# A decoder layer on one core: expert choice one step later in the dense stage, and a new order of the tail

## What is computed

```python
cat = concatenate([_rms_norm(attn_o, g_attn), _rms_norm(conv_o, g_conv)])
h = _layer_norm(ALPHA * x + cat @ w_out, ln1_g, ln1_b)

scores = sigmoid(h @ router_w)                      # 64 experts, 8 groups of 8
sel = scores + router_bias
gscore = sum(top_k(sel.reshape(T, 8, 8), 2))        # per group
emask = groups among the top 4 by gscore
eidx = top_k(where(emask, sel, -inf), 6)
w = scores[eidx] / sum(scores[eidx]) * 2.5
routed = sum over the six experts of w * (silu(h @ w_gate[e]) * (h @ w_up[e])) @ w_down[e]
shared = (silu(h @ ws_gate) * (h @ ws_up)) @ ws_down
y = _layer_norm(ALPHA * h + routed + shared, ln2_g, ln2_b)
```

## Time and profile before

| | |
|---|---|
| median of 3 runs | 2155.15 us (2153.55 to 2159.5) |
| the profiled execution, its own time | 2160.44 us |
| its span, from first to last instruction | 2158.7 us |
| mean granted TensorE clock | 0.983 of full speed |
| PE busy | 2056.4 us, 95% of the span |
| DVE busy | 1412.8 us, 65% |
| ACT busy | 1244.0 us, 58% |
| POOL busy | 635.8 us, 29% |
| chain that ended last, PE's part | 38% of the span |

### The profile page before, as it was taken

The page is one execution under the profiler, slowest core; times in us unless marked ns, Lnnn a source line. Parts: engine busy times, 40 slices in busy tenths (PEclk is TensorE's granted clock), DMA queues, the critical chain, the costliest instruction groups (busy, mean ns, idle before and its releaser), DMA issues.

```text
span 2158.7 us, 37047 instructions
## 1 busy us (share of the span) xinstructions
PE 2056.4 (95%) x11574; PEld 1728.6 (80%) x11574; DVE 1412.8 (65%) x2788; ACT 1244.0 (58%) x2169; POOL 635.8 (29%) x659
## 2 busy tenths in 40 slices
PE   8999999999989999969999999999999999999984
PEld 6777787787767777758888888898988888888773
DVE  6444444444667777776777777677767777767657
ACT  6344344343543444436777777677667777766655
POOL 2111111111013332442534444445443333333200
PEclk9999999999999999989999999999999999999997
DMA  5101101010463433467999999999999999999983
GB/s 218 60 31 37 44 30 37 31 39 32 174 240 130 143 129 133 141 218 218 299 296 301 281 311 284 281 298 286 295 286 290 290 295 289 287 279 280 293 311 120
DMA packets 118605, 433.78 MB, mean 201 GB/s; under 512 B 36272, under 2 KB 40880, under 8 KB 90192
## 3 DMA queue, kind: packets, MB, share of 16 engines
q1 hardware_dynamic: 80656, 309.94, 39.0%
q0 software_dynamic: 37872, 122.90, 24.3%
HBM read 328.44 MB, written 106.51 MB: 201 GB/s over the span
## 4 chain that ended last, share of the span: by engine, by line
PE 38%; DMA 6%; issue 4%; POOL 4%; ACT 1%; DVE 1%; DVEq 1%; SPq 0%; POOLq 0%; ACTq 0%
PE ex_psU L2190 15%; PE ex_psU L2192 7%; PE ex_psX L2176 4%; PE ex_psY L2170 4%; PE ex_psY L2168 4%; PE ex_psY L2169 4%; DMA entries<-table 4%; POOL acc_d L1773 2%; POOL ex_xg L1790 1%; DMA ex_xg<-h_d,entries 1%; PE ex_psY L2221 1%; DMA acc_d<-ex_y,ex_rows 1%; DMA ex_t<-acc_d 1%; POOL ex_rows L1766 0%; ACT ex_scratch L1930 0%
## 5 line engine op out<-in xcount | busy, mean ns | idle before, releaser
L2190 PE MATMUL ex_psU<-ex_xs,ex_guh 128*128 128x384 f32 (+5 forms) x2016 | 624.6, 373 | 3.5 <-issue 3.4
L2192 PE MATMUL ex_psU<-ex_xs,ex_gul 128*128 128x192 f32 (+5 forms) x2016 | 523.6, 260 | 0.0
L2190 PEld LDWEIGHTS ex_psU<-ex_xs,ex_guh 128*128 128x128 f32 x2016 | 379.3, 188 | 53.2 <-issue 21.4
L2192 PEld LDWEIGHTS ex_psU<-ex_xs,ex_gul 128*128 128x128 f32 x2016 | 385.2, 191 | 1.4
L1790 POOL DMA_INDIRECT ex_xg<-h_d,entries x128 | 158.0, 1234 | 481.8 <-issue 220.9
L1773 POOL DMA_INDIRECT acc_d<-ex_y,ex_rows x128 | 216.3, 1690 | 199.5 <-ACT ex_y L1853 153.2
L1853 ACT ACTIVATE ex_y<-ex_psY,ex_use 128x512 f32<-128x512 f32 (+5 forms) x256 | 171.1, 682 | 41.9 <-PE ex_psY L2221 26.1
L1985 DVE TENSOR_TENSOR ex_gu<-ex_psU,ex_lo 128x512 f32<-128x512 f32 (+5 forms) x136 | 82.7, 608 | 171.8 <-ACT ex_lo L1813 171.7
L2168 PE MATMUL ex_psY<-ex_dnh,ex_hdh 128*128 128x512 f32 (+3 forms) x432 | 179.4, 415 | 9.2 <-DVE ex_hdl L2002 5.8
L1813 ACT ACTIVATE ex_lo<-ex_psU 128x512 f32<-128x512 f32 (+5 forms) x136 | 71.6, 527 | 181.5 <-PE ex_psU L2192 172.9
L2014 DVE TENSOR_TENSOR ex_xs<-ex_psX,ex_xs 128x512 fp32r<-128x512 f32 (+5 forms) x125 | 130.6, 1045 | 65.5 <-ACT ex_xs L1842 64.7
(11 more groups left out here) (413 smaller groups left out, 4259.1 us busy)
## 6 DMA issues: line engine op xcount, KB each, us to landing
mi_g_raw<-w_experts SPq DMA_DIRECT2D x96, 1024.0 KB, 8.1
mi_g_place<-w_experts SPq DMA_DIRECT2D x96, 1024.0 KB, 8.0
mi_xr<-xT SPq DMA_DIRECT2D x17, 512.0 KB, 3.6
acc_d<-de_acc SPq DMA_DIRECT2D x17, 512.0 KB, 2.9
h_d<-de_h POOLq DMA_DIRECT2D x17, 512.0 KB, 3.8
de_cr<-cat SPq DMA_DIRECT2D x16, 512.0 KB, 4.3
de_xr<-x_rows SPq DMA_DIRECT2D x16, 512.0 KB, 3.7
hT_d<-de_hT SPq DMA_DIRECT2D x8, 1024.0 KB, 3.9
```

Of the source, the lines that this page charges most:

```text
L2190: nc.tensor.matmul(psU[:, f, half, 0:2 * n].rearrange("p (s n) -> p s n", s=2), guh[:, b, kc, c0:c0 + P], rows_split(e)[:, kc, :, 0:n], st ...
L2192: last = nc.tensor.matmul(psU[:, f, half, 0:n], gul[:, b, kc, c0:c0 + P], rows_split(e)[:, kc, 0, 0:n], start=False, stop=(kc == KC - 1))
```

## The change

In the dense stage `pick` moves from the end of step i to the next step, between `split_h` and `ranks`. On TensorE `rank` and `router` move into the shared expert's work: behind half of `down` in even steps, behind five of the eight chunks of `gate_up` in odd steps. The end of the stage is rewritten alike. In the tail the three products of a block go into one PSUM range of 256 columns, so `copy_lo` and `sums` fall away there, and ScalarE's sigmoid and VectorE's multiplies read PSUM; TensorE then waits for the second multiply (s_hid) instead of for the sum. The norms are made in another order, with four batches in place of six.

The lists that set the order of the norms:

```diff
-STATS = (1, 3, 5, 0, 2, 7, 9, 4, 6, 11, 13, 15, 16, 8, 10, 12, 14)
-BATCHES = (3, 5, 9, 13, 15, 17)
+STATS = (1, 3, 0, 2, 5, 7, 4, 6, 9, 11, 13, 15, 16, 8, 10, 12, 14)
+BATCHES = (4, 10, 15, 17)
```

VectorE, dense step:

```diff
                 else:
+                    pick(i - 1)
                     ranks(i - 1)
...
                 if k == 1:
                     activate(m, psU)
-                pick(i)
...
             split_h(LAST - 1, psT[:])
+            pick(LAST - 2)
             ranks(LAST - 2)
-            place(LAST - 2)
             residual(LAST)
             normalise(LAST, 2, True)
+            place(LAST - 2)
+            split_h(LAST, psA[:])
             pick(LAST - 1)
-            split_h(LAST, psA[:])
             activate(SHARED - 2, psU)
```

TensorE, dense step (not the first):

```diff
                     project(i + 1, 1 - k, 1)
+                    pe.wait_ge(S["hT_lo"], i + 1)
                     if k == 0:
                         pe.wait_ge(S["hid_lo"], m + 1)
-                    rank(i - 1)
-                    pe.wait_ge(S["hT_lo"], i + 1)
-                    if k == 0:
-                        down(m, psT)
-                router(i)
-                if k == 1:
-                    after(pe, S["hid"], m)
-                    gate_up(psU[:], range(KC)).then_inc(S["gu"], 1)
+                        down(m, psT, (0,))
+                        rank(i - 1)
+                        router(i)
+                        down(m, psT, (1,)).then_inc(S["down"], 1)
+                    else:
+                        after(pe, S["hid"], m)
+                        gate_up(psU[:], range(0, 5))
+                        rank(i - 1)
+                        router(i)
+                        gate_up(psU[:], range(5, KC)).then_inc(S["gu"], 1)
                 logits(i)
```

ScalarE, tail: head of the new order, and the chain:

```diff
-            def chain(n, f, first=lambda: None, second=lambda: None):
-                copy_lo(e + n, f, BLK)
-                first()
-                sigmoid(e + n, f, BLK)
-                second()
+            def chain(n, f):
+                act.wait_ge(s_gu, 2 * (e + n) + f + 1)
+                act.wait_ge(s_hid, 2 * (e + n) + f)
+                A(lo[:, 0, :], psU[:, f, 0, 0:BLK], ACT.Sigmoid).then_inc(s_sig, 1)
                 hidden(e + n, f, n % 2, BLK)
...
             statistics(1)
             statistics(3)
-            statistics(5)
+            squares(0)
+            squares(2)
             deviations(0)
             chain(1, 1)
-            squares(0)
-            squares(2)
-            deviations(1)
+            statistics(5)
             chain(2, 0)
```

VectorE, tail: the chain:

```diff
-                sums(e + n, f, BLK)
-                activate(e + n, f, n % 2, BLK)
+                gate, up = psU[:, f, 0, 0:BLK], psU[:, f, 1, 0:BLK]
+                dve.wait_ge(s_sig, 2 * (e + n) + f + 1)
+                V.tensor_tensor(gu[f][:, 1, :], gate, lo[:, 0, :], ALU.mult)
+                dve.drain()
+                V.tensor_tensor(gu[f][:, 0, :], gu[f][:, 1, :], up, ALU.mult).then_inc(s_hid, 1)
```

TensorE, tail: gate_up_block:

```diff
-                pe.wait_ge(s_sum, 2 * (e + n) + f - 1)
+                if n == 0:
+                    pe.wait_ge(s_sum, 2 * e + f - 1)
+                else:
+                    pe.wait_ge(s_hid, 2 * (e + n) + f - 1)
...
-                        nc.tensor.matmul(psU[:, f, half, :].rearrange("p (s c t) -> p s c t", s=2, c=2), guh[:, 0, kc, c0:c0 + P],
-                                         x[:, :, kc].rearrange("p c s t -> p s c t"), start=(kc == 0), stop=False)
-                        last = nc.tensor.matmul(psU[:, f, half, 0:BLK].rearrange("p (c t) -> p c t", c=2), gul[:, 0, kc, c0:c0 + P],
-                                                x[:, :, kc, 0, :], start=False, stop=(kc == KC - 1))
+                        hi, lo = guh[:, 0, kc, c0:c0 + P], gul[:, 0, kc, c0:c0 + P]
+                        last = three(out, hi, lo, x[:, :, kc, 0, :], x[:, :, kc, 1, :], kc == 0, kc == KC - 1)
```

More of the change, by code:

```diff
@@ L1462, in hidden_T, with down @@
                 last.then_inc(S["hidT"], 1)
-            def down(m, out):
+            def down(m, out, halves=range(2)):
                 pe.wait_ge(S["hid_lo"], m + 1)
-                for hf in range(2):
+                for hf in halves:
                     cols = slice(hf * 512, (hf + 1) * 512)
@@ L1470, in down @@
                                      f == 0, f == FC - 1)
-                last.then_inc(S["down"], 1)
+                return last
             def router(i):
@@ L1545, in _ @@
             rank(LAST)
-            down(SHARED - 2, psA)
+            down(SHARED - 2, psA).then_inc(S["down"], 1)
             hidden_T(LAST, SHARED - 1, psU)
@@ L1752, in _ @@
             load_tiles(5)
-            for n, i in enumerate(ON_DVE):
+            for n, i in enumerate(FINISH):
                 sp.wait_ge(s_out, n + 2)
@@ L2107, in _ @@
             centre(3)
-            centre(5)
+            centre(0)
+            centre(2)
+            chain(1, 1)
             reciprocals(0)
@@ L2111, in _ @@
             finish(3)
-            chain(1, 1)
-            finish(5)
-            centre(0)
-            centre(2)
-            reciprocals(1)
+            chain(2, 0)
             finish(0)
             finish(2)
-            chain(2, 0)
+            centre(5)
             add(1, 0)
             add(1, 1)
+            centre(7)
             centre(4)
             centre(6)
-            centre(7)
+            chain(2, 1)
             centre(9)
-            reciprocals(2)
+            centre(11)
+            reciprocals(1)
+            finish(5)
+            chain(3, 0)
+            finish(7)
             finish(4)
-            chain(2, 1)
             finish(6)
-            finish(7)
-            chain(3, 0)
-            finish(9)
-            centre(11)
+            chain(3, 1)
             centre(13)
-            chain(3, 1)
             add(2, 0)
             add(2, 1)
+            finish(9)
+            finish(11)
             centre(15)
             centre(16)
-            reciprocals(3)
-            finish(11)
-            finish(13)
-            add(3, 0)
-            finish(16)
-            finish(15)
             centre(8)
             centre(10)
-            reciprocals(4)
+            add(3, 0)
+            reciprocals(2)
+            finish(13)
+            finish(15)
+            add(3, 1)
+            finish(16)
             finish(8)
-            add(3, 1)
             finish(10)
@@ L2153, in _ @@
             centre(14)
-            reciprocals(5)
+            reciprocals(3)
             finish(12)
```

30 lines of the change are left out of this document (16 added, 14 removed).

## The result

The changed kernel takes 2188.68 us (median of 4 runs, 2184.76 to 2191.8), the kernel before 2156.11 us beside it (4 runs, 2153.55 to 2159.5): a ratio of 1.0149, with a 95% interval of 1.0127 to 1.0171. It is slower by 32.6 us; the forecast was 28 us slower (2183 us, range 2168 to 2199). The profiled execution took 2189.05 us with a span of 2187.3 us, 28.6 us over the span before.

| stretch | before | after | difference | forecast |
|---|---|---|---|---|
| to the first projection of the loop | 624.62 | 624.57 | 0 | 0 |
| seven turns of the dense loop | 272.55 | 312.58 | +40.0 | +34.5 (26.5 waits, 8 clock) |
| last projection to the experts | 56.34 | 66.60 | +10.3 | +5 |
| experts | 1099.39 | 1088.74 | -10.6 | 0 |
| first block product to the end | 105.80 | 94.81 | -11.0 | -11.5 |

What follows compares the result with a forecast made beforehand. It took TensorE to bound the dense loop, a VectorE chain close behind, and VectorE the tail. Waits 26.5 + clock 5 and 8 for stage end and clock - tail 11.5 = +28 us on 2155.15: 2183 us, range 2168 to 2199.

Steps and rivals of the forecast that it cites:

- The loop's waits: Dense loop: later rank product delays the next projection through VectorE's 6.50 us chain, +3.79 us a turn, +26.5 us in seven.
- The clock: Dense loop: TensorE's clock falls after half of fourteen idle times, less two falls there now, +8 us (-3 to +20).
- Rival 1: Dense loop: the clock falls at most gaps, total +40 us, 2195 us; chance 0.12.
- The end of the stage: Behind the dense loop: pick of tile 15 between split_h and ranks delays the last router, +5 us (+3 to +8).
- Pick late at no cost: Dense loop, VectorE: the projection and first gate-up chunks cover the later pick, cost nothing; 7 us kept for the range.
- The tail: Last stretch, bound by VectorE: shorter activation chains (5.9 us) and new order of norms, together -11.5 us (-6 to -17).
- Three products of 256 columns at 0: Tail, TensorE: 128 more instructions for the same columns, 0 to +4 us, hidden in idle time, taken as 0.
- Rival 4: Tail, TensorE: the third product's weight loads are not hidden, 24 us, idle time taking about half, 2195 us; chance 0.04.
- what would show it: Profile signs: 42 us turns, waits before projection and router, none before logits, later experts, five to nine low-clock stretches, shorter tail.
- Rival 2: Dense loop: moved work fills TensorE's 2.26 us of waits a turn if rank to split_cat fits behind, 2128 us; chance 0.09.
- Rival 3: Tail: transfers bind, so it gains only 4 us, 2191 us; chance 0.06.

Runs made afterwards that it cites:

- e7: Kernel before with only TensorE's rank and router moved amid the shared work in the dense loop, pick where it was: 2193.4 us, ratio 1.016.
- e4: Changed kernel with VectorE's split_cat moved between pick and ranks in each dense step: 2154.38 us, ratio 0.9992 to the kernel before.
- e8: Kernel before with only the end of the dense stage, behind the loop, rewritten as in the changed kernel: 2161.01 us, ratio 1.0024.
- e6: Kernel before with only VectorE's pick moved later, in the loop and for tile 14, TensorE's order kept: 2175.45 us, ratio 1.0074.
- e10: Kernel before with the tail's three products in one PSUM range and the short activation chain, old order of norms: 2148.73 us, ratio 0.9979.
- e11: Kernel before with split_cat ahead of ranks, only the router amid shared work, rank directly behind the projection, and the changed tail: 2126.47 us, ratio 0.9888.
- e2: Kernel before with only the tail part of the change, dense stage as before: 2138.59 us, ratio 0.9911.
- e3: Kernel before with VectorE's split_cat moved ahead of ranks and residual in each dense step: 2143.9 us, ratio 0.9938.
- e5: Changed kernel with eight throw-away products of 512 columns before each projection of the dense loop: 2176.88 us, ratio 1.0077 to the kernel before.
- e12: e11 with place of tile 14 behind the last normalise, and ranks of tile 15 and all gate-up chunks earlier: 2117.8 us, ratio 0.983.

## Why the forecast was right, point by point

- **The loop's waits: right.** +3.81 us a turn (41.98 - 38.17) against +3.79, by the mechanism forecast: e7 has it with TensorE's part alone, and in e4 the wait for the low part goes when split_cat leaves the chain (other waits leave 1.3 us a turn). The steps were forecast at 20.10 and 21.86 us and took 20.11 and 21.87. The two idle times were put at 3.1 and 2.5 us and are 2.83 and 2.15, since TensorE's work there was put too low: the rank product's own 0.23 us was left out, and the logits count 0.55 us before an idle time, not 0.37. This changes the idle time, not the step. (Half of 2.95 us is 1.475, not 1.44; it makes no difference here.)
- **The clock: right mechanism, mis-sized.** The term was "half of fourteen", +8 us; it measures +13 to +14 us in the loop. After ten of the fourteen gaps the clock fell, not after seven. Most falls had about the price of the forecast (44.95 - 41.98 = 2.97 us for two), but two were longer: the steps from 715.57 and 848.88 us took 24.7 us in place of 21.87, 2.8 to 2.9 us each. Rival 1, "most gaps", was nearer the fact, and its 2195 us is as far from the result as the forecast is. The range held both.
- **The end of the stage: the moves right, the clock left out.** +5 us was the term, and +10.3 was measured. Pick between split_h and ranks was put at 4.5 us and measures 4.3; all the moves measure +6.7 us in e8 against the one execution of before, +5.3 against the mean of the four with that end. The rest is clock, a term that I had taken for the loop alone: 3.5 us between e8 and the changed kernel.
- **Pick late at no cost: right for the changed order only.** The text had the mask at 757.0 us and the rank product at 758.2, 1.2 us of slack in the odd step; in the changed kernel the mask is done at 772.9 and the rank product starts at 775.78, 2.9 us later, and in the even step the slack is 1 us (753.0 and 753.92). In e6, where rank isn't late, pick costs 2.04 us a turn. The slack was real, and it came from the move of the rank product.
- **The tail: right.** -11.0 us against -11.5. Over more executions it is slightly more: six with the old tail took 105.4 to 109.1 us, six with the new one 93.5 to 94.9, 12.4 us between the means. The chain was put at 5.9 us and measures 6.4 (e10, which keeps all six batches of reciprocals); the order, with four batches, measures 7.0 alone. By steps: the multiply of chain(1,1) was to come 33.1 us into the tail and came at 2126.84 - 2092.49 = 34.4 (37.8 before); the down product behind it was to wait 1.5 us and waited 1.8; the wait of 4.22 us of the earlier trace rows is gone. TensorE's wait for the adds of block 2 grew from 2.9 us to 4.5 us. The two waits of the changed kernel:

```profile
PE ex_psY L2172 <- DVE ex_stats L2083: 4.5, 1, 4.5
PE ex_psY L2172 <- DVE ex_hdl L2005: 1.8, 1, 1.8
```

- **Three products of 256 columns at 0: right.** Rival 4 (24 us, half of it on the path) needed 0.19 us a load in the open; the spacing is 0.12 us. The rule of the Trainium skill (TensorE: Matmul & The Clock Gate, The mechanism), that a load overlaps a product only where it goes to other rows of the array, doesn't describe this tail: by it rival 4 would have come true. The same section also lets a load go ahead of running products into a background weight buffer, and with that the spacing of 0.12 us agrees; no run here shows where the loads go.
- **The experts: not foreseen.** The forecast started from one execution, and that one had 8.6 us of waits for gathers. It put the sum against the median, 5.3 us lower, but carried no term for what the other execution would have there. With experts of equal length the two traces would have differed by 39 us, not 28. The medians of single parts say the same: the dense part costs 46 us (37 to 53) for a forecast of 39.5, the tail part gives 19 us (13 to 25) for a forecast of 11.5, and the two errors cancel in part.
- **Of what would show it:** turns of 42 us, 0.48 us before every router, no wait before logits and the shorter tail were there. The experts started 50 us later, not 35 to 40, and there were eleven low-clock stretches, not five to nine: ten in the loop (the first, at its start, is there in the kernel before too) and one behind its last gap. The clock is most of both.
- **The rivals.** Rival 2 named the point that decides, and the experiments could move the kernel across it: the path from rank to split_cat is 6.5 us and doesn't fit, but with split_cat taken off it all three waits go (e11, turns of 35.8 us, 2.4 us less for rival 2's 2.3), there with pick and rank in their old places and only the router moved. Rival 3 fell with e2, whose tail takes 93.9 us.

## What to carry to other kernels

When a small product is moved later in a stream that is nearly full, ask first what stands behind its reader on the other engine: here a call that didn't depend on the ranks at all, split_cat, stood behind them in VectorE's queue. Moving that call ahead gave 12 us in the kernel before; moving the product later cost 40 us in the loop. A gap costs its length and then the clock: fourteen gaps of 2 to 3 us cost half as much again here, seven of 1.31 us cost 3 us, and gaps up to 1.2 us cost nothing behind the loop's first step. Before a stage whose transfers vary is taken as fixed, look at it in more than one execution.

## What the hardware did that was not expected

- Idle times of equal length and cause don't have equal effect on the clock. In the changed loop it fell after ten of fourteen gaps of 2.15 or 2.83 us, and stayed high after gaps of both lengths (740.31 and 760.42 in the rows above). In e3, e5, e11 and e12 it didn't fall in the loop once its first step was over; the gaps there were up to 1.2 us, but for one of 1.52 us in e3. With seven of 1.31 us, in the kernel before, it fell twice, and with seven of 2.0 us, in e4, three times.
- Eight throw-away products in each gap gave 19 us back over the loop and made the kernel 11.8 us faster in the medians (e5; in its profiled execution the experts with 1094.1 us and the work ahead of the loop took back 8.6 us).
- The experts' length varied by 12 us over the fourteen profiled executions, with waits for gathers in the long ones. The tail of before took 105.4 to 109.1 us in six executions, and the end of its dense stage 56.2 to 59.9 us in four, with the granted clock at 0.91 to 0.83.
